# Expert stage of a hybrid decoder step: a subtraction moved from VectorE to GpSimd, a fifth gather buffer, and gather work spread 13 to 13

## The reference, cut to what matters

```python
a = jax.nn.gelu(jnp.einsum('td,thkd->thk', tb, u_tab[e]).astype(jnp.float32), approximate=False)
return jnp.einsum('thk,thkd->td', (g * a).astype(tb.dtype), v_tab[e])
```

## Time and profile before

| what | us |
|---|---|
| median of 3 runs | 3903.67 |
| lowest, highest run | 3901.28, 3909.6 |
| the profiled execution | 3909.41 |
| its span, first to last instruction | 3907.8 |
| PE, PEld busy | 3267.4, 2846.2 |
| DVE, ACT, POOL busy | 2644.8, 1348.8, 1591.6 |
| mean granted TensorE clock | 0.929 of full speed |

### The profile page before, as it was taken

The page is one execution under the profiler, slowest core; times in us unless marked ns, Lnnn a source line. Parts: engine busy times, 40 slices in busy tenths (PEclk is TensorE's granted clock), DMA queues, the critical chain, the costliest instruction groups (busy, mean ns, idle before and its releaser), DMA issues. The chain is left out here.

```text
span 3907.8 us, 58722 instructions
## 1 busy us (share of the span) xinstructions
PE 3267.4 (84%) x20561; PEld 2846.2 (73%) x20561; DVE 2644.8 (68%) x5883; ACT 1348.8 (35%) x3194; POOL 1591.6 (41%) x1343
## 2 busy tenths in 40 slices
PE   6999788566687975656699999999999999999994
PEld 3676455211277964555599999999999999999993
DVE  4224776110234799989688888888888888888885
ACT  3010566000221113879433323333323333333331
POOL 0010000000212444999645545545546455455450
PEclk8999899777788987888899999999999999999997
DMA  6632873999412122665688888888888888888883
GB/s 226 239 131 73 236 215 114 367 414 410 165 65 89 60 76 71 251 245 204 273 311 332 314 311 340 321 320 339 306 327 322 317 335 316 315 336 312 320 293 136
DMA packets 280369, 991.41 MB, mean 254 GB/s; under 512 B 21925, under 2 KB 139536, under 8 KB 215865
## 3 DMA queue, kind: packets, MB, share of 16 engines
q1 hardware_dynamic: 214648, 480.71, 34.0%
q0 software_dynamic: 62784, 469.88, 31.8%
q10 hardware_dynamic: 2752, 38.75, 2.6%
HBM read 909.52 MB, written 146.80 MB: 270 GB/s over the span
## 5 line engine op out<-in xcount | busy, mean ns | idle before, releaser
L2210 PE MATMUL e_pa<-k_hi_d,e_uh 128*128 128x320 f32 x2048 | 616.0, 314 | 77.7 <-DVE e_act L2371 62.1
L2211 PE MATMUL e_pa<-k_lo_d,e_uh 128*128 128x320 f32 x2048 | 605.5, 309 | 0.0
L2410 POOL DMA_INDIRECT e_uv<-peer_uv,k_g_idx x416 | 400.6, 963 | 498.2 <-DVE e_pY L2351 442.5
L2339 DVE CUSTOM_DVE_ANT_0 e_uv<-e_uv,e_h 128x1024 f32<-128x1024 f32 x416 | 504.2, 1212 | 61.3 <-DMA e_uv<-peer_uv,k_g_idx 60.6
L2351 DVE SCALAR_TENSOR_TENSOR e_pY<-e_uv,e_wts,e_pY 128x1024 f32<-128x1024 f32 x412 | 527.3, 1280 | 0.0
L2210 PEld LDWEIGHTS e_pa<-k_hi_d,e_uh 128*128 128x128 f32 x2048 | 385.5, 188 | 103.6 <-DVE e_act L2371 87.7
L2405 POOL TENSOR_TENSOR e_vl<-e_v,e_vh 128x1024 fp32r<-128x1024 f32 x128 | 308.9, 2413 | 294.5 <-ACT e_vh L2262 294.0
L2289 ACT ACTIVATE e_gel<-e_dots 128x1 f32<-128x1 f32 x416 | 83.4, 200 | 956.2 <-DVE e_dots L2339 953.4
L2232 PE MATMUL e_po<-e_ph,e_vh 128*128 128x320 f32 x2048 | 387.4, 311 | 16.8 <-DVE k_OT L2385 12.3
L2211 PEld LDWEIGHTS e_pa<-k_lo_d,e_uh 128*128 128x128 f32 x2048 | 385.7, 188 | 0.0
L2241 PE MATMUL e_po<-e_pl,e_vh 128*128 128x320 f32 x2048 | 384.0, 309 | 0.4
(11 more groups left out here) (332 smaller groups left out, 5868.9 us busy)
## 6 DMA issues: line engine op xcount, KB each, us to landing
k_kv<-kv_pages SPq DMA_DIRECT2D x128, 512.0 KB, 6.7
s_kv<-kv_state SPq DMA_DIRECT2D x32, 2048.0 KB, 17.3
e_v<-peer_uv SPq DMA_DIRECT2D x128, 512.0 KB
e_u<-peer_ut SPq DMA_DIRECT2D x126, 512.0 KB
s_g<-r_G SPq DMA_DIRECT2D x10, 4096.0 KB
k_OT<-s_g SPq DMA_DIRECT2D x64, 640.0 KB
v_win_sample<-state_v_win POOLq DMA_DIRECT2D x28, 1168.0 KB
k_win_sample<-state_k_win ACTq DMA_DIRECT2D x28, 1168.0 KB
```

What stands on the lines that cost most here:

```text
L2210: nc.tensor.matmul(pa[:, m % 2, 0:WD], uh[:, c % 2, k], keep.hi_d[:, k, cols], start=(k == 0), stop=False)
L2211: nc.tensor.matmul(pa[:, m % 2, 0:WD], uh[:, c % 2, k], keep.lo_d[:, k, cols], start=False, stop=False)
L2339: nc.vector.tensor_tensor_reduce(uv[:, r, 0:D], uv[:, r, 0:D], h[:], 1.0, 0.0, ALU.mult, ALU.add, dots[:, r:r + 1]).then_inc(row_dotted, 1)
L2410: nc.gpsimd.indirect_dma_start(uv[:, s % RING], None, io["peer_uv"], bass.IndirectOffsetOnAxis(ap=keep.g_idx[:, s:s + 1], axis=0),).then_i ...
```

## The change

- The low part `e_pl` is formed on GpSimd (`low_p`) in place of VectorE, in each of the eight slots beside the dots, ahead of `low_v` where the slot has one. VectorE's multiplication n waits in addition for `e_pl` n - 2, since `e_act` has two buffers.
- `RING` is 5. The two row buffers `e_hrow` and `e_grow` are gone; one row in two parts (768 and 256 columns) lies in memory that this stage doesn't need, and serves both. So each copy and each DMA of a row is two, the load of the tokens of tile t + 1 waits for the store of the sums before it, and it is issued at the ninth step of a tile.
- The table: 13 gather operations beside the dots and 13 beside the sums (11 and 15 before).

```diff
-RING = 4
+RING = 5
+HEAD = 768
...
-        hrow = sb("e_hrow", [P, D])[:]
-        grow = sb("e_grow", [P, D])[:]
+        hrow = (keep.rest[:, KC * T - KC * DT - HEAD:KC * T - KC * DT],
+                keep.mod[:].rearrange("p m s -> p (m s)")[:, 0:D - HEAD])
+        parts = (slice(0, HEAD), slice(HEAD, D))
...
-        BESIDE = (2, 2, 2, 1, 2, 1, 1, 0) + (0,) + (1,) * (OUTS - 1)
+        BESIDE = (2, 2, 2, 2, 2, 2, 1, 0) + ((0,) + (1,) * 4) * 2 + (0,) + (1,) * 5
...
                 def h_load(t):
-                    act.dma_start(hrow, io["s_h"][t]).then_inc(h_in, 16)
+                    for row, part in zip(hrow, parts):
+                        act.dma_start(row, io["s_h"][t][:, part]).then_inc(h_in, 16)
 
                 def h_copy(t):
-                    act.wait_ge(h_in, 16 * t + 16)
-                    nc.scalar.activation(h[:], hrow, ACT.Copy).then_inc(h_ready, 1)
-                    if t < GP:
-                        act.wait_ge(h_ready, t + 1)
-                        h_load(t + 1)
+                    act.wait_ge(h_in, 32 * t + 32)
+                    for row, part in zip(hrow, parts):
+                        x = nc.scalar.activation(h[:, part], row, ACT.Copy)
+                    x.then_inc(h_ready, 1)
+                    if t == 0:
+                        act.wait_ge(h_ready, 1)
+                        h_load(1)
...
+                            if s % P == 8 and 0 < tile_of(s) < GP:
+                                act.wait_ge(grow_out, 32 * tile_of(s))
+                                h_load(tile_of(s) + 1)
                         s = sums_of(NR * i + j)
                         if s is not None and last_of(s):
                             t = tile_of(s)
                             act.wait_ge(row_added, s + 1)
-                            if t:
-                                act.wait_ge(grow_out, 16 * t)
-                            nc.scalar.activation(grow, pY[:], ACT.Copy).then_inc(grow_done, 1)
+                            if t < GP:
+                                act.wait_ge(h_ready, t + 2)
+                            else:
+                                act.wait_ge(grow_out, 32 * t)
+                            for row, part in zip(hrow, parts):
+                                x = nc.scalar.activation(row, pY[:, part], ACT.Copy)
+                            x.then_inc(grow_done, 1)
                             act.wait_ge(grow_done, t + 1)
-                            act.dma_start(io["s_go"][t], grow).then_inc(grow_out, 16)
+                            for row, part in zip(hrow, parts):
...
-                    ops = share(m)
+                    if n >= 2:
+                        v.wait_ge(pl_done, n - 1)
                     v.wait_ge(g_in[c // 2], 16 * i + 16)
                     v.wait_ge(gelu_done, n + 1)
                     nc.vector.tensor_tensor(act_out[:, m % 2].rearrange("p (h t) -> p h t", h=ND),
                                             pa[:, m % 2, 0:WD].rearrange("p (h t) -> p h t", h=ND),
                                             Gt[:, c // 2, ND * b:ND * (b + 1), c % 2], ALU.mult).then_inc(p_done, 1)
-                    gathers(i, ops[:1])
-                    v.wait_ge(ph_done, n + 1)
-                    nc.vector.tensor_tensor(pl[:, c, cols], act_out[:, m % 2], ph[:, c, cols], ALU.subtract).then_inc(pl_done, 1)
-                    gathers(i, ops[1:])
+                    gathers(i, share(m))
...
+                def low_p(i, m):
+                    n, c, b = DOTS * i + m, m // NBD, m % NBD
+                    cols = slice(b * WD, (b + 1) * WD)
+                    pool.wait_ge(ph_done, n + 1)
+                    nc.gpsimd.tensor_tensor(pl[:, c, cols], act_out[:, m % 2], ph[:, c, cols], ALU.subtract).then_inc(pl_done, 1)
...
                         if m % NBD == 1 and m // NBD < 2:
                             low_u(CQ * i + 2 + m // NBD)
+                        low_p(i, m)
                         if m in V_AT:
                             low_v(CQ * i + V_AT.index(m))
                         gathers(i, m)
```

More of the change, by code:

```diff
@@ L2303, in gathers @@
                             act.wait_ge(row_added, s + 1)
-                            if t:
-                                act.wait_ge(grow_out, 16 * t)
-                            nc.scalar.activation(grow, pY[:], ACT.Copy).then_inc(grow_done, 1)
+                            if t < GP:
[5 more added lines that the diff above has]
+                            x.then_inc(grow_done, 1)
                             act.wait_ge(grow_done, t + 1)
-                            act.dma_start(io["s_go"][t], grow).then_inc(grow_out, 16)
+                            for row, part in zip(hrow, parts):
+                                act.dma_start(io["s_go"][t][:, part], row).then_inc(grow_out, 16)
                 act.dma_start(uu[:, 0], uview[0]).then_inc(u_in[0], 16)
@@ L2327, in _ @@
                         gathers(i, DOTS + n)
-                act.wait_ge(grow_out, 16 * (GP + 1))
+                act.wait_ge(grow_out, 32 * (GP + 1))
             @block.vector
```

## The result

The changed kernel takes **3955.65 us** in the median of four runs (3951.96 to 3959.82), the kernel before 3904.65 beside it: a ratio of 1.0132, with a 95% interval of 1.0116 to 1.0148. It is slower by 51 us, where 3900 was forecast and 3935 was the upper end. The profiled execution's span is 3956.0 us (3907.8 before).

What follows compares the result with a forecast made beforehand. TensorE was taken as the bound, with 3.34 us of stops a round; 31 x (59.58 - 59.66) - 2.1 + 0.4 + 0.5 = -3.7 us put the median at 3900, own range 3889 to 3911, whole range 3870 to 3935.

Steps and rivals of the forecast that it cites:

- (4): TensorE at the out groups: waits for the fourth e_vl and slot 6's e_pl; stops 3.26 us, not 3.34, round 59.58.
- (1): VectorE beside the dots: without the subtraction its cycle falls from 4.21 to 3.81 us and no longer stops TensorE.
- (2): GpSimd, eight subtractions a round ahead of e_vl: 0.88 us each at 320 elements, bounds 0.75 and 1.07.
- (3): GpSimd's queue beside the dots: 26.26 us from the first e_vl, so slot 6's e_pl ends 32.53 into the round.
- (5): Five gather places: gathers issued 7.3 us or more ahead of their dots; GpSimd's lateness hides late ones, so those waits vanish.
- (6): Loads and split rows: no load later; extra copies and DMA issues cost +0.4 us at the start, +0.5 at the end.
- (7): First round: loses the 2.40 us block ahead of the first gelu cycle, -2.1 us (0 to -2.4).
- Cheaper: Subtraction on GpSimd at 0.75 us each: 0.78 us a round less, 24 us, 3876 us; chance 0.14.
- dearer GpSimd: Subtraction on GpSimd at 1.07 us: 35 us more, 3935; with a dearer gather behind it 50 us; chance 0.17.
- Full relief: TensorE has no stop left in the expert stage: 105.5 us gained, 3798 us; chance 0.04.
- The fourth: VectorE's L2371 or L2385 waits for an e_pl on GpSimd: 1.2 us of stop, 3903 us; chance 0.03.

Runs made afterwards that it cites:

- the kernel with the early e_vl: The changed kernel with each round's first e_vh and e_vl formed at the end of the round before, the other three one step earlier: 3849.06 us.
- the fastest one: The kernel with the early e_vl, plus slot 5's gather behind slot 6's e_pl and the gather table turned to dot, then sum, in a slot: 3803.33 us.
- the kernel with one stop: The changed kernel with only the gather of slot 5 moved behind the e_pl of slot 6 in GpSimd's queue: 3886.53 us.

## Why the prediction was wrong

**The step that failed is (4)**, its last line: "Then 4 x 0.147 and 15 out groups follow". The 0.147 a matmul is read from a stretch in which TensorE had not stopped. Behind the two stops it holds in 6 rounds of 31; in the others the first quartets run at 0.27, and a round costs 1.5 us more (2.4 to 2.9 in four). A term for the clock is missing from the sum, and from the rivals: none of the four had it, so the range ended at 3935, by the price of one subtraction. The upper end should have been 31 x 1.5 higher. In the stage before there was no fall to see: its stops of 3.34 us a round were scattered, 1.01 the largest in the earlier trace rows, and the clock was 1.00. Larger ones were there, but single. This is the largest, 1.69 in front of the matmul and 1.85 from start to start less 0.147, with the stretch around it:

```profile
3120.53 0.41 PE L2210 MATMUL e_pa<-k_hi_d,e_uh 128*128 128x320 f32 x1 [1.69 <-DVE e_act L2371]
...
3119.00:3128.00 9.00, 7.04 (x46) 6.78 (x47) 7.03 (x8) 4.71 (x11) 5.80 (x3) 1.00 0.75 293
```

The sum took "the stops of 3.34 become 3.26, in another place" for the same price. It wasn't: the new ones, 1.90 and 1.41, stand in one place with 0.59 of work between them. The granted clock outside the stage was in the profile's page, at 0.929 for the whole execution, and should have made a rival: from 684 to 1075 us, where TensorE is busy for 60%, it is 0.77.

Point by point:

- (1) VectorE's cycle without the subtraction: forecast 3.81, measured 3.84. Right. TensorE's stops beside the dots are gone.
- (2) e_pl at 320 columns: forecast 0.88, measured 0.885. Right, by the slope of two neighbouring sizes. The estimate of 0.69 from the Trainium skill's figure is refuted.
- (3) The end of GpSimd's queue: forecast 32.53, measured 32.59. Right.
- (4) The stops: 1.8 and 1.4 forecast; the rows' 1.37 and 1.15 of idle time count from the modelled end of the matmul ahead, start to start they are 2373.46 - 2370.97 - 0.59 = 1.90 and 2375.46 - 2373.46 - 0.59 = 1.41. Right; what follows them, wrong, as above.
- (5) Gathers no longer wait while GpSimd is late: 4.7 us. Right for this kernel. "If GpSimd weren't late, they would show" is so in part: with five places they are 21.3 us in 31 waits in the kernel with the early e_vl and 1.9 in the fastest one. Only with four places are they large (184.9).
- (6), (7) The ends: forecast -2.1 + 0.4 + 0.5, measured -0.4 for the first round and +1.2 behind the last one. About 2 us too hopeful, and small.
- Rivals. Cheaper and dearer GpSimd: excluded by 0.885. Full relief: not in this kernel, but the fastest of the experiments reached 3803, where that rival said 3798. The fourth, that VectorE now waits for GpSimd: L2385 keeps 0.49 us in all 256, of which 148 lie wholly inside one of GpSimd's operations. It reads one input from PSUM. The subtraction that reads two from SBUF is blocked, for up to 2.53, in the kernel that keeps it on VectorE, in the 64 of 256 that start inside an e_ul on GpSimd.

The Trainium skill has a rule that bears on the missing term ("TensorE: Matmul & The Clock Gate", What's actually happening): the low clock is the default, and recent activity releases it; the gate's monitor runs freely, so that its phase against the work varies. The traces are in line with both: filled stops keep the clock at 1.00, and in the changed kernel the same stops come out with either clock, 1.00 or 0.79 over the same 8.1 us of a round (shown at the end). At the 1.5 us that a fall costs in these rows, one in every round would have added 46 us to the sum: 3947 instead of 3900.

## What to carry to other kernels

A stop of TensorE has two prices: its own length, and what the matmuls behind it cost at half the clock. The second price was 1.5 us where nothing but TensorE set the pace behind the stop, and next to nothing where TensorE would have waited again (62.82 us a round with and without a fall). When a change gathers small scattered stops into one place, sum them there and put a clock term beside them as a rival, even if their total falls. And when work moves to an engine with room on average, look at the part of the round in which it is full: most of the gain came when one e_vl left that half and the dot was placed so that ScalarE's steps ran beside the sum; moving one gather there was worth 18 us of the 102.

## What the runs showed of the hardware

- Stops of 1.90 and 1.41 us with 0.59 of work between them were followed by the low clock in 25 rounds of 31. A single stop of about 1.9 was in 8 of 31. One of 2.6 was in 18 of 31, in the kernel with the subtraction back on VectorE. The stops of the kernel before were not (1.2 in nearly every round, 1.85 the largest), nor were those of 0.3 to 1.9, mostly below 1.1, of the kernel with the early e_vl.
- The stops don't decide it alone. In the changed kernel, the round at 2221.87 has two stops like those of the round at 2342.81 and keeps the full clock. The windows 28.19 to 36.29 into each:

```profile
2250.06:2258.16 8.10, 5.40 (x34) 4.78 (x34) 3.01 (x5) 2.13 (x4) 7.74 (x7) 1.00 0.96 370
2371.00:2379.10 8.10, 5.47 (x23) 4.71 (x23) 2.20 (x4) 2.21 (x4) 7.74 (x7) 0.79 1.01 412
```

- What decides between two equal rounds was not tried. That the falls of the kernel with one stop are evenly spaced, and all begin 31.8 to 32.3 us into their round, speaks for a rhythm of the chip against that of the rounds. So does the changed kernel: from its sixth round to its eleventh the low stretch begins some 0.17 later each time, 32.71 to 33.58 into the round, and the twelfth has none. It is argued, not shown.
- A fifth place of 8 KB in each partition is worth 146 us in a kernel that is otherwise almost free of stops.
